# Recurrent heads of a hybrid block: PSUM sums in three sets of banks in turn instead of two

## The chip, the cores and the metric

The kernel runs on one core of one Trainium2 chip. Times are device microseconds (us) of the whole program, from one launch; lower is better. The core has TensorE (PE in the profile, with its weight loads as PEld), VectorE (DVE), ScalarE (ACT), GpSimd (POOL) and SyncE (SP, here a queue of DMA issues). TensorE writes its results into PSUM, 8 banks of 512 fp32 values per partition; ACT and DVE read them from there.

## The reference, cut to what matters

Two layers of a diffusion transformer over 1280 tokens (256 of context, 1024 latent), width 1024. The first layer has an S5 branch and a gated linear recurrence (RG-LRU) with 4 heads of 256 channels; the change is in the latter.

```python
# per head of 256 channels; h: [1280, 1024]
xr, gr = h @ w_xr, h @ w_gr                    # two projections
xc = centred_dwconv(xr, conv_w, conv_b)        # 4 taps over time
for d in (forward, backward):
    r  = sigmoid(xc @ wa[d] + ba[d])           # gates, 256x256 each
    ig = sigmoid(xc @ wx[d] + bx[d])
    a  = exp(-8 * r * softplus(-lam[d]))
    b  = sqrt(1 - a*a) * ig * xc
    h_t = a_t * h_(t-1) + b_t                  # a scan over the tokens
out = (forward + backward) * silu(gr)
```

## The kernel before

Each engine has a program written out by hand, with semaphores between them; nothing is reordered by a planner. The recurrent heads are one stage of the program, four heads one after another in a loop (`RH` = 4); they take about 442 us of the whole.

A head has twelve **sums** on PE. A sum is one tile of 128 channels by 1280 tokens, accumulated in PSUM in three pieces of 512, 512 and 256 tokens (`SEGS`), 2.5 banks in all. I number them j = 0 to 11 in the order of PE's program:

- sums 0 and 1: the projection `xr` for the two halves s of the head (8 steps of k for each piece, signal `rg_pmm`);
- sums 2 and 3: the projection `gr` (the same size);
- sums 4 to 11: for u = 0 to 3 (direction d, half s), the gate sums m = 0 (r) and m = 1 (ig), 2 steps of k for each piece, signal `rg_gmm`.

Even sums go to `ps3[0]` (banks 0, 1 and half of bank 2), odd sums to `ps3[1]` (banks 3, 4 and half of bank 5). Banks 6, 7 and the other halves of 2 and 5 are not used in this stage. PE may start sum j only when sum j-2 has been taken out of the same set: that is `pe.wait_ge` on `rg_ev0` or `rg_ev1` (lines 965 and 979). These two semaphores rise by 6 in each head: once by ACT's copy of sum 0 or 1, once by DVE's product of sum 2 or 3 with its own sigmoid, and four times by ACT's sigmoids of the gate sums.

What the other engines do for a head, in their program's order:

- ACT: waits for the end of the head before (`rg_bo`), because `xrp` and the gate `SG` lie in one place; copies sums 0 and 1 into `xrp` (L1554, L1555); waits for both halves of the convolution (`xc_ready`); takes the sigmoids of sums 2 and 3 (L1559); then for each u the two sigmoids of the gate sums (L1570), the square root for u-1 (L1562, in `root`), an exponential, a square and a tanh (L1574, L1578, L1579). Changes between these functions cost table loads.
- DVE: after the last product of the head before (L2297, signal `rg_bo`) 10 steps of the S5 scan (`scan_steps`, 4 small operations each, L2239 to L2244), the convolution of half 0 (L2260 to L2264), 8 steps, the convolution of half 1, 2 steps, the product of sum 2 with its sigmoid (L2269, `rg_ev0`), 1 step, the product of sum 3 (`rg_ev1`), 5 steps, and then for each u `gated(u)` (L2276, L2278) and `recurrence(u)` (L2287 and the token scans L2289 to L2297).
- POOL runs the other half of the S5 scan beside all that. SP loads weights.

PE waits for `xc_ready` and the gate weights before sum 4. After the last head PE goes on with `gate_rows` (banks 4 to 6, L1590 takes them) and `outputs`.

Of the kernel before, what the change touches and what calls it, by code (L numbers as in the profile page):

```python
# [17 lines left out]
ALU = mybir.AluOpType  # L18
ACT = mybir.ActivationFunctionType
AX = mybir.AxisListType  # L20

P = 128
BANK = 512
D = 1024
DT = D // P
CTX, LAT = 256, 1024
TOK = CTX + LAT
SEGS = [(0, 512), (512, 512), (1024, 256)]
# [10 lines left out]
NB = G // GB  # L39
# [8 lines left out]
RH, RD = 4, 256  # L48
# [9 lines left out]
LOFF = CTX + 3  # L58
# [45 lines left out]
def build(nc, A, out):  # L104
    with ExitStack() as ctx:
# [13 lines left out]
        def sem(name):  # L119
            name = lineage(name)[0]  # L120
            if name not in sems:
                sems[name] = ctx.enter_context(nc.semaphore(name))
            return sems[name]

        def past(name, n):

            return sem(name), n + lineage(name)[1]
# [7 lines left out]
        def mm(o, lhsT, rhs, k, n):  # L135
            return nc.tensor.matmul(o, lhsT, rhs, start=(k == 0), stop=(k == n - 1))  # L136
# [5 lines left out]

        psf = ps[:, :, :].rearrange("p b c -> p (b c)")
        ps3 = [psf[:, 3 * s * BANK:3 * s * BANK + TOK] for s in range(2)]

        def at(o, n):
            return AR[:, o:o + n]
# [5 lines left out]
        PV = sb("param_cols", 384)  # L153
# [13 lines left out]
        Wv = W[:, :].rearrange("p (s k n) -> p s k n", s=2, k=DT)  # L167
# [123 lines left out]
        xrp = rb(0, 2 * PAD).rearrange("p (s t) -> p s t", s=2)  # L291
        xcb = rb(2572, 2 * TOK).rearrange("p (s t) -> p s t", s=2)
# [5 lines left out]
        SG = rb(0, 2 * TOK).rearrange("p (s t) -> p s t", s=2)  # L298
# [25 lines left out]
        GWv = GW[:, :].rearrange("p (d m k n) -> p d m k n", d=2, m=2, k=2)  # L324
# [30 lines left out]
        HT = over("h_full", DT * TOK, AR0 + 4 * HTo, F32)[:, :].rearrange("p (k t) -> p k t", k=DT)  # L355
# [475 lines left out]
        def _(pe):  # L831
# [31 lines left out]
            for k in range(2, DT):  # L863
                c, h = 1 + (k - 2) // 2, 4 * (k % 2)
# [4 lines left out]
            for b in range(NBLK):  # L869
                last = mm(ps[:, 6, b:b + 1], sq_sum0[:, P * b:P * b + P], ones[:, 0:1], 0, 1)  # L870
            last.then_inc(sem("ss_mm0"), 1)
            pe.wait_ge(*past("mod_row", 5))
            for (c0, n), row in zip(MODC, mod_rows):
                for b in range(0, n, P):
                    g = 2 * ((c0 + b) // P)
                    last = nc.tensor.transpose(ps[:, 4, g:g + 2], row[:, b:b + P], ident[0:2, 0:2])
            last.then_inc(sem("mod_cols"), 1)
            pe.wait_ge(*past("diag0", 1))
            for b, (o, n) in ((0, (ps[:, 5, 0:CTX], 2)), (2, (ps[:, 6], 4)), (6, (ps[:, 7], 4))):
                last = mm(o, ones[:, :], diag0[:, b:b + n].rearrange("p b c -> p (b c)"), 0, 1)  # L880
# [18 lines left out]
            for k in range(DT):  # L899
                pe.wait_ge(*past("h_low", k + 1))  # L900
                for m in range(2):
                    last = u_product(m, k)
                    if k == DT - 1:
                        last.then_inc(sem(f"u_mm{m}"), 1)
            for m in range(2, DT):
                i, s = m // 2, m % 2
                pe.wait_ge(*past("u_wl", m - 1))
                pe.wait_ge(*past(f"u_ev{s}", i))
                for k in range(DT):
                    last = u_product(m, k)  # L910
# [16 lines left out]
            with pe.Fori(0, NB // 2) as i:  # L927
                for s in range(2):
# [3 lines left out]
                    for r in range(2):  # L932
                        for g in range(GB):
# [6 lines left out]
                            last = mm(ps[:, r, P * g:P * g + P], Xw[s][r][:, P * g:P * g + P], (nident, ident)[r][:, :], 1, 2)  # L940
                    last.then_inc(sem(f"x_t{s}"), 1)
                    for g in range(GB):
                        for d in range(2):
                            rw = slice(64 * d, 64 * d + 64)
                            for r in range(2):
                                last = mm(ps[0:HC, 6 + d, P * g:P * g + P], BBv[rw, s, r, :, g],
                                          Gv[s][rw, g, r, d:d + T, :], r, 2)
# [5 lines left out]
                    for r in range(2):  # L953
                        for g in range(GB):
                            last = mm(ps[:, 2 + 2 * r + g // 2, NJ * (g % 2):NJ * (g % 2) + NJ], Eg[:, r, g], Ub[s][:, g], 0, 1)
# [3 lines left out]
            pe.wait_ge(*past("h_back2", 3))  # L959

            def branch_head(i):
                for kind in range(2):
                    for s in range(2):
                        pe.wait_ge(*past(f"rg_w{s}", 32 * i + 16 * kind + 16))
                        pe.wait_ge(*past(f"rg_ev{s}", 6 * i + kind))
                        for t0, n in SEGS:
                            if isinstance(i, int) and kind == 0 and s == 0 and t0 == 1024:
                                pe.wait_ge(*past("wz_a", NB))
                                pe.wait_ge(*past("wz_v", NB))
                                pe.wait_ge(*past("v_ev", NB))  # L970
                            for k in range(DT):
                                last = mm(ps3[s][:, t0:t0 + n], Wv[:, s, k], HT[:, k, t0:t0 + n], k, DT)
                        last.then_inc(sem(f"rg_pmm{s}"), 1)
                pe.wait_ge(*past("rg_gw", 64 * i + 64))
                pe.wait_ge(*past("xc_ready", 2 * i + 2))
                for u in range(4):
                    d, s = u // 2, u % 2
                    for m in range(2):
                        pe.wait_ge(*past(f"rg_ev{m}", 6 * i + (2 + u)))
                        for t0, n in SEGS:  # L980
                            for k in range(2):
                                last = mm(ps3[m][:, t0:t0 + n], GWv[:, d, m, k, P * s:P * s + P], xcb[:, k, t0:t0 + n], k, 2)
                        last.then_inc(sem(f"rg_gmm{m}"), 1)

            branch_head(0)
            with pe.Fori(1, RH) as i:
# [2 lines left out]
            def gate_rows(i, z, js):  # L989
                for j in js:  # L990
                    t0, n = SEGS[j]
                    pe.wait_ge(*past(f"gs_w{z}", 16 * i + 16))
                    pe.wait_ge(*past(f"gs_ev{j}", 2 * i + z))
                    for k in range(DT):
                        last = mm(ps[:, 4 + j, 0:n], Wv[:, z, k], HT[:, k, t0:t0 + n], k, DT)
                    last.then_inc(sem(f"gs_mm{z}"), 1)
# [30 lines left out]
            def modulation_columns():  # L1027
# [6 lines left out]
                        last = mm(o, mod1_rows[z][:, x + P * t:x + P * t + P], quads[:, 0:n], 0, 1)  # L1034
                last.then_inc(sem("mod1_cols"), 1)

            gate_rows(0, 0, (2,))
            pe.wait_ge(*past("rg_ev0", 6 * RH))
            pe.wait_ge(*past("rg_ev1", 6 * RH))
# [25 lines left out]
            with pe.Fori(0, DT // 2) as i:  # L1065
                for s in range(2):
                    pe.wait_ge(*past("glu_wl", 2 * i + (s + 1)))
                    pe.wait_ge(*past(f"glu_sz{s}", i))
                    for k in range(DT):
                        pe.wait_ge(*past("y_low", k + 1))  # L1070
                        last = three_parts(ps3[s], WPs[s], YTs, k, DT)
# [72 lines left out]
            for k in range(DT):  # L1144
                pe.wait_ge(*past("ht1_low", k + 1))
                for s in range(2):
                    for q, (a, b) in enumerate(PARTS):
                        for j, (t0, n) in enumerate(XSEGS[s]):
                            last = mm(psP[s][j], WXs[s][:, a, k], HTs[b][:, k, t0:t0 + n], 3 * k + q, 3 * DT)
# [9 lines left out]
            for g in range(GQ):  # L1159
                last = nc.tensor.matmul(quarter(g), WFs[:, 0, 0], X2[:, 0, GN * g:GN * g + GN], start=True, stop=False, skip_group_check=True)  # L1160
# [244 lines left out]
        def _(act):  # L1405
# [144 lines left out]
            with act.Fori(0, RH) as i:  # L1550
                act.wait_ge(*past("rg_bo", 2 * i))
                for s in range(2):
                    act.wait_ge(*past(f"rg_pmm{s}", 2 * i + 1))
                    nc.scalar.activation(xrp[:, s, 1:1 + CTX], ps3[s][:, 0:CTX], ACT.Copy)  # L1554
                    nc.scalar.activation(xrp[:, s, LOFF + 1:LOFF + 1 + LAT], ps3[s][:, CTX:TOK], ACT.Copy).then_inc(sem(f"rg_ev{s}"), 1)  # L1555
                act.wait_ge(*past("xc_ready", 2 * i + 2))
                for s in range(2):
                    act.wait_ge(*past(f"rg_pmm{s}", 2 * i + 2))
                    nc.scalar.activation(SG[:, s], ps3[s], ACT.Sigmoid).then_inc(sem("rg_sg"), 1)  # L1559
                def root(u):  # L1560
                    act.wait_ge(*past("rg_om", 4 * i + (u + 1)))
                    nc.scalar.activation(RT[:, u % 2], RT[:, u % 2], ACT.Sqrt).then_inc(sem("rg_sq"), 1)  # L1562

                for u in range(4):
                    d, s = u // 2, u % 2
                    if u >= 2:
                        act.wait_ge(*past("rg_dir", 4 * i + (u - 1)))
                    for m, (dst, c0) in enumerate(((RT, C_BA), (IT, C_BX))):
                        act.wait_ge(*past(f"rg_gmm{m}", 4 * i + (u + 1)))
                        nc.scalar.activation(dst[:, s], ps3[m], ACT.Sigmoid, bias=PV[:, bass.ds(2 * i + (c0 + 8 * d + s), 1)]).then_inc(sem(f"rg_ev{m}"), 1)  # L1570
                    if u:
                        root(u - 1)
                    act.wait_ge(*past("rg_ev0", 6 * i + (3 + u)))
                    nc.scalar.activation(AT[:, s], RT[:, s], ACT.Exp, scale=lamc[:, bass.ds(2 * i + (8 * d + s), 1)]).then_inc(sem("rg_at"), 1)  # L1574
                    act.wait_ge(*past("rg_at", 12 * i + (3 * u + 1)))
                    if u:
                        act.wait_ge(*past("rg_om", 4 * i + u))
                    nc.scalar.activation(TT[:, 0:TOK], AT[:, s], ACT.Square).then_inc(sem("rg_at"), 1)  # L1578
                    nc.scalar.activation(RT[:, s], RT[:, s], ACT.Tanh, scale=lamc[:, bass.ds(2 * i + (16 + 8 * d + s), 1)]).then_inc(sem("rg_at"), 1)  # L1579
                root(3)  # L1580
# [237 lines left out]
            for m in range(MT):  # L1818
# [5 lines left out]
                if m == 0:  # L1824
# [6 lines left out]
                    for n, r in enumerate((rLI, rLF)):  # L1831
                        nc.scalar.activation(r[0:32], psG[64 * n:64 * n + 32], ACT.Identity, bias=BI[64 * n:64 * n + 32, :])
                        for o, x in zip(natural(r, slice(32, 64)), (psG[64 * n + 32:64 * n + 64, 0:CTX], psG[64 * n + 32:64 * n + 64, CTX:TOK])):
                            last = nc.scalar.activation(o, x, ACT.Identity, bias=BI[64 * n + 32:64 * n + 64, :])
# [130 lines left out]
        def _(dve):  # L1965
            V = nc.vector
# [20 lines left out]
            for q in range(24):  # L1987
                t0, n = SEGS[q % 3]
# [135 lines left out]
            f, bk = slice(0, 64), slice(64, 128)  # L2124
# [100 lines left out]
            with dve.Fori(0, RH) as i:  # L2225
                k, step = [0], [0]
# [39 lines left out]
                for s in range(2):  # L2266
                    scan_steps(1)
                    dve.wait_ge(*past("rg_sg", 2 * i + s + 1))
                    V.tensor_tensor(SG[:, s], ps3[s], SG[:, s], ALU.mult).then_inc(sem(f"rg_ev{s}"), 1)  # L2269
                scan_steps(5)  # L2270

                def gated(u):
# [149 lines left out]
            with dve.Fori(0, MT // 2) as i:  # L2422
                k = [0]
# [583 lines left out]
```

## Time and profile before

| | us |
|---|---|
| time, median of 3 runs (lowest to highest) | 2696.11 (2691.78 to 2697.48) |
| the profiled execution: its time | 2691.36 |
| its span, first to last instruction | 2689.7 |
| mean granted clock of TensorE | 0.983 of 2.4 GHz |
| PE busy | 2550.7 (95% of the span) |
| DVE / ACT / POOL busy | 1530.1 / 827.5 / 988.3 |

The profiled execution lies at the fast end of the runs; 1.7 us of its time lie outside its span. A share of busy time is a mean over stages with different limits, so the stage of the heads is read by itself. An fp32 matmul shows as two records. The line of most matmuls is L136, a helper, so they are told apart by their operands: `h_full,weights` are the projections, `arena,weights` 128x128 are the gate sums.

### The profile page before, as it was taken

To read this page: it belongs to the slowest core of one execution; us is meant where nothing else is said; L and a number is where in the kernel's file an instruction comes from. 1 tells how busy PE (TensorE), PEld (TensorE's weight loads), DVE (VectorE), ACT (ScalarE), POOL (GpSimd) and SP (SyncE) were. 2 spreads that over 40 slices of the span, in tenths; PEclk is the share of its full clock that TensorE was granted. 3 is DMA by queue.
4 is the path that set the end of the run, shared out by engine and by line. 5 is a ranking of instruction groups with operands and counts; after the bars stand their busy time and mean duration, and the time that the engine had idled before them with its cause. 6 is when DMAs were issued, how large, how long until landed. Compare 5 with 4: busy or idle time off the path is not lost.

```text
span 2689.7 us, 37273 instructions
## 1 busy us (share of the span) xinstructions
PE 2550.7 (95%) x13319; PEld 1979.7 (74%) x13319; DVE 1530.1 (57%) x2359; ACT 827.5 (31%) x994; POOL 988.3 (37%) x1162
## 2 busy tenths in 40 slices
PE   7898899999999998999999999998999999999998
PEld 3787854545455667888877887777989889898787
DVE  3677765887875225524246664966465555646510
ACT  2425635263552113312122112123233241422210
POOL 0139967887800100211224433445334333331000
PEclk9999999999999999999989999999999999999999
DMA  7413320111106785351132333564131321215421
GB/s 295 121 57 92 97 76 27 48 32 43 51 16 215 252 266 157 100 183 36 36 98 95 124 117 125 177 230 153 44 116 54 106 88 63 100 35 173 133 94 47
DMA packets 272083, 293.95 MB, mean 109 GB/s; under 512 B 35232, under 2 KB 234184, under 8 KB 271568
## 3 DMA queue, kind: packets, MB, share of 16 engines
q1 hardware_dynamic: 202672, 209.75, 24.3%
q10 hardware_dynamic: 64672, 65.70, 7.4%
q0 software_dynamic: 4608, 16.78, 1.9%
q8 instruction: 79, 1.29, 0.2%
q14 instruction: 52, 0.43, 0.1%
HBM read 200.99 MB, written 91.20 MB: 109 GB/s over the span
## 4 chain that ended last, share of the span: by engine, by line
PE 69%; DVE 9%; issue 3%; ACT 3%; DMA 2%; POOL 1%; ACTq 0%; SPq 0%; DVEq 0%; POOLq 0%
PE ps L136 61%; PE ps L1372 6%; DVE xc_part L2536 1%; PE ps L1023 1%; ACT arena L1570 1%; DVE arena L2464 1%; ACT L1570 1%; DMA ml_z<-arena 0%; PE ps L1377 0%; DVE arena L528 0%; PE ps L1305 0%; DMA qk_map_full<-ml_qk_maps 0%; DVE arena L2453 0%; PE ps L1203 0%; DVE arena L2465 0%
## 5 line engine op out<-in xcount | busy, mean ns | idle before, releaser
L136 PE MATMUL ps<-h_full,weights 128*128 128x512 f32 (+1 forms) x1152 | 417.8, 523 | 8.7 <-ACT arena L1570 4.0
L136 PE MATMUL ps<-h_part,in_weight_parts 128*128 128x512 f32 (+1 forms) x1920 | 412.8, 376 | 13.7 <-POOL in_weight_parts L2879 6.5
L136 PEld LDWEIGHTS ps<-h_part,in_weight_parts 128*128 128x128 f32 x1920 | 337.0, 190 | 84.6 <-issue 8.1
L136 PEld LDWEIGHTS ps<-h_full,weights 128*128 128x128 f32 x1152 | 218.3, 190 | 201.5 <-issue 187.0
L136 PE MATMUL ps<-v_part,p_part 128*128 128x512 f32 x1248 | 296.7, 396 | 0.1
L136 PEld LDWEIGHTS ps<-v_part,p_part 128*128 128x128 f32 x1248 | 235.4, 191 | 49.6 <-issue 0.8
L136 PE MATMUL ps<-q_part,xc_part 128*128 128x256 f32 x1920 | 244.4, 286 | 3.9 <-DVE q_part L2569 3.9
L136 PEld LDWEIGHTS ps<-q_part,xc_part 128*128 128x128 f32 x1920 | 234.1, 192 | 4.9 <-DVE q_part L2569 4.5
L136 PE MATMUL ps<-arena,weights 64*16 64x128 f32 (+2 forms) x896 | 177.3, 388 | 16.0 <-ACT arena L1570 14.4
L1372 PE MATMUL ps<-wo_part,mx_part 128*128 128x512 f32 x768 | 183.9, 400 | 5.2 <-DVE mx_part L2536 4.8
L2873 POOL TENSOR_TENSOR in_weight_parts<-weights,ones 128x1024 fp32r<-128x1024 f32 x32 | 81.3, 2541 | 258.3 <-PE ps L136 188.0
L1372 PEld LDWEIGHTS ps<-wo_part,mx_part 128*128 128x128 f32 x768 | 145.4, 191 | 39.8 <-issue 5.0
L2959 POOL TENSOR_TENSOR decays<-decays,p_full 128x256 f32<-128x256 f32 (+1 forms) x128 | 150.6, 1177 | 60.4 <-DVE p_full L2647 34.8
L136 PEld LDWEIGHTS ps<-arena,weights 64*16 64x16 f32 (+1 forms) x896 | 101.1, 144 | 89.4 <-issue 64.3
L2375 DVE SCALAR_TENSOR_TENSOR arena<-ps,modulation,arena 128x256 f32 (+3 forms) x32 | 32.6, 1061 | 164.5 <-PE ps L136 160.6
L136 PE MATMUL ps<-y_part,out_weight_parts 128*128 128x512 f32 (+1 forms) x576 | 113.0, 358 | 3.5 <-DVE y_part L2321 2.3
L136 PE MATMUL ps<-bo_part,out_weight_parts 128*128 128x512 f32 (+1 forms) x576 | 114.6, 359 | 0.0
L136 PE MATMUL ps<-ao_part,out_weight_parts 128*128 128x512 f32 (+1 forms) x576 | 114.4, 358 | 0.0
L136 PEld LDWEIGHTS ps<-y_part,out_weight_parts 128*128 128x128 f32 x576 | 95.0, 188 | 21.4 <-DVE y_part L2321 2.7
L136 PEld LDWEIGHTS ps<-ao_part,out_weight_parts 128*128 128x128 f32 x576 | 95.3, 188 | 16.9
L136 PEld LDWEIGHTS ps<-bo_part,out_weight_parts 128*128 128x128 f32 x576 | 95.3, 188 | 16.9
L136 PE MATMUL ps<-arena 128*128 128x160 f32 (+4 forms) x620 | 98.2, 297 | 6.4 <-DMA arena<-s_lags 6.0
(396 smaller groups left out, 4119.1 us busy)
## 6 DMA issues: line engine op xcount, KB each, us to landing
weights<-in_e_w_in SPq DMA_DIRECT2D x32, 512.0 KB, 5.1
weights<-in_o_w_in SPq DMA_DIRECT2D x32, 512.0 KB, 4.5
arena<-in_mod_w POOLq DMA_DIRECT2D x24, 512.0 KB, 5.6
ml_xcv<-arena ACTq DMA_DIRECT2D x16, 640.0 KB, 2.9
xc_full<-ml_xcv SPq DMA_DIRECT2D x4, 2560.0 KB, 10.5
xm_tiles<-ml_xm SPq DMA_DIRECT2D x15, 640.0 KB, 3.8
arena<-in_mod_w SPq DMA_DIRECT2D x4, 2048.0 KB, 21.3
s_out_maps<-arena ACTq DMA_DIRECT2D x32, 256.0 KB, 3.3
```

The source lines that it names most:

```text
L136: return nc.tensor.matmul(o, lhsT, rhs, start=(k == 0), stop=(k == n - 1))
L1023: last = nc.tensor.matmul(ps[32 * g:32 * g + 32, 7, o:o + MN], csw[:, k], modw1[n % 3][:, x:x + MN], start=(n % MU1 == 0), stop=(k == DT - ...
L1372: nc.tensor.matmul(ps[:, 2 * (b % 4) + h], Mbs[x][b % 2][:, k], Wos[w][k][:, BANK * h:BANK * h + BANK], start=(k == 0 and n == 0), stop=Fa ...
L1570: nc.scalar.activation(dst[:, s], ps3[m], ACT.Sigmoid, bias=PV[:, bass.ds(2 * i + (c0 + 8 * d + s), 1)]).then_inc(sem(f"rg_ev{m}"), 1)
L2375: V.scalar_tensor_tensor(out=o, in0=a, scalar=MOD[:, bass.ds(4 * i + (2 * (16 + s) + w), 1)], in1=x, op0=ALU.mult, op1=ALU.add).then_inc(s ...
L2464: V.scalar_tensor_tensor(out=bst2[:, s], in0=xcz[:, s], scalar=PV[:, C_SK + m:C_SK + m + 1], in1=zo[:, s], op0=ALU.mult, op1=ALU.mult)
L2536: V.tensor_tensor(o, x, h.bitcast(F32), ALU.subtract).then_inc(sem(name), 1)
L2873: GP.tensor_tensor(WXs[s][:, 0], Wv[:, s], ones[:, :].unsqueeze(1).to_broadcast([P, DT, P]), ALU.mult).then_inc(sem("w_high"), 1)
L2959: GP.tensor_tensor(Sp[:, z, s0:s1], Sp[:, z, s0:s1], PR[:, z, o:o + s1 - s0], ALU.add).then_inc(sem("sums"), 1)
```

## The change

The sums of a head take three sets of banks in turn. Set A (j mod 3 = 0) begins in the second half of bank 5 and covers banks 6 and 7; set B (j mod 3 = 1) is banks 0, 1 and half of 2, set C (j mod 3 = 2) banks 3, 4 and the first half of 5. So sets A and C share bank 5, each with a piece of 256 tokens; in set A the order of pieces is 256-767, 768-1279, 0-255, so that in both the piece in the shared bank comes third. Sum j starts when sum j-3 has been taken. Before its third piece a sum in set A also waits until sum j-1 (set C) has been taken, and a sum in set C until sum j-2 (set A) has been. ACT gets two waits for the first gate sums (u = 0), and the rows after the last head one more. ACT and DVE read the sums from their new places; no operation is added, removed or put elsewhere in their order.

```diff
+        RG_AT = (5 * BANK + 256, 0, 3 * BANK)
+        rg_ps = [psf[:, RG_AT[j % 3]:RG_AT[j % 3] + TOK] for j in range(12)]
+        RG_SEGS = [((256, 512), (768, 512), (0, 256)), SEGS, SEGS]
...
             def branch_head(i):
+                def sums_taken(j):
+                    c = (j % 12 if j < 0 else j) // 2 + (1 if j >= 0 else -5)
+                    if not (isinstance(i, int) and 6 * i + c <= 0):
+                        pe.wait_ge(*past(f"rg_ev{j % 2}", 6 * i + c))
+
+                def rg_sums(j, product, steps):
+                    sums_taken(j - 3)
+                    for x, (t0, n) in enumerate(RG_SEGS[j % 3]):
+                        if x == 0 and isinstance(i, int) and i == 0 and j == 0:
+                            pe.wait_ge(*past("v_ev", NB))
+                        if x == 2 and isinstance(i, int) and i == 0 and j == 0:
+                            pe.wait_ge(*past("wz_a", NB))
+                            pe.wait_ge(*past("wz_v", NB))
+                        if x == 2 and j % 3 == 0:
+                            sums_taken(j - 1)
+                        if x == 2 and j % 3 == 2:
+                            sums_taken(j - 2)
+                        for k in range(steps):
+                            w, v = product(k, t0, n)
+                            last = mm(rg_ps[j][:, t0:t0 + n], w, v, k, steps)
+                    return last
...
-                        pe.wait_ge(*past(f"rg_ev{s}", 6 * i + kind))
...
+                        rg_sums(2 * kind + s, lambda k, t0, n: (Wv[:, s, k], HT[:, k, t0:t0 + n]), DT).then_inc(sem(f"rg_pmm{s}"), 1)
...
-                        pe.wait_ge(*past(f"rg_ev{m}", 6 * i + (2 + u)))
...
+                        rg_sums(4 + 2 * u + m, lambda k, t0, n: (GWv[:, d, m, k, P * s:P * s + P], xcb[:, k, t0:t0 + n]), 2).then_inc(sem(f"rg_gmm{m}"), 1)
...
+            pe.wait_ge(*past("rg_ev1", 6 * RH - 1))
             gate_rows(0, 0, (2,))
...
-                    nc.scalar.activation(SG[:, s], ps3[s], ACT.Sigmoid).then_inc(sem("rg_sg"), 1)
+                    nc.scalar.activation(SG[:, s], rg_ps[2 + s], ACT.Sigmoid).then_inc(sem("rg_sg"), 1)
...
+                        if u == 0:
+                            act.wait_ge(*past(f"rg_ev{m}", 6 * i + 2))
-                        nc.scalar.activation(dst[:, s], ps3[m], ACT.Sigmoid, bias=...
+                        nc.scalar.activation(dst[:, s], rg_ps[4 + 2 * u + m], ACT.Sigmoid, bias=...
...
-                    V.tensor_tensor(SG[:, s], ps3[s], SG[:, s], ALU.mult).then_inc(sem(f"rg_ev{s}"), 1)
+                    V.tensor_tensor(SG[:, s], rg_ps[2 + s], SG[:, s], ALU.mult).then_inc(sem(f"rg_ev{s}"), 1)
```

## Rows read from the trace of the kernel before

**Rows 1.** Busy time by engine, stretches of one head; the second head and the sum of four.

```profile
core 0: us, PE busy (x) PEld busy (x) DVE busy (x) ACT busy (x) POOL busy (x), PEclk, DMA share, GB/s
469.50:581.50 112.00, 108.39 (x288) 56.12 (x288) 92.86 (x201) 52.59 (x43) 90.33 (x180) 0.95 0.11 36
...
sum 442.00, PE 421.83 PEld 220.32 DVE 336.01 ACT 198.91 POOL 306.17; mean PE 105.46 PEld 55.08 DVE 84.00 ACT 49.73 POOL 76.54
```

**Rows 2.** Waits in the stage (359 to 806 us): total, times, longest.

```profile
PE ps L136 <- ACT arena L1570: 18.5, 10, 2.8
...
PE ps L136 <- DVE arena L2269: 1.5, 1, 1.5
```

**Rows 3.** PE in order of time: start, duration, line, operands, records, idle before.

```profile
359.16 68.98 PE L136 MATMUL ps<-h_full,weights 128*128 128x512 f32 x192 [2.65 <-DMA weights<-in_e_w_in]
427.98 17.35 PE L136 MATMUL ps<-arena,weights 128*128 128x512 f32 x48
446.13 8.86 PE L136 MATMUL ps<-arena,weights 128*128 128x512 f32 x24 [0.80 <-ACT arena L1570]
457.80 8.86 PE L136 MATMUL ps<-arena,weights 128*128 128x512 f32 x24 [2.81 <-ACT arena L1570]
...
540.02 17.35 PE L136 MATMUL ps<-arena,weights 128*128 128x512 f32 x48
...
652.06 17.45 PE L136 MATMUL ps<-arena,weights 128*128 128x512 f32 x48 [1.54 <-DVE arena L2269]
...
762.50 17.35 PE L136 MATMUL ps<-arena,weights 128*128 128x512 f32 x48
...
801.01 3.62 PE L136 MATMUL ps<-h_full,weights 128*128 128x256 f32 x16
...
820.64 17.42 PE L136 MATMUL ps<-h_full,weights 128*128 128x512 f32 x48 [1.42 <-ACT weights L1590]
```

**Rows 4.** ACT in order of time, gate sums of the first head.

```profile
444.75 2.54 ACT L1570 ACTIVATE arena<-ps,param_cols 128x1280 f32<-128x1280 f32 x2
...
456.42 2.55 ACT L1570 ACTIVATE arena<-ps,param_cols 128x1280 f32<-128x1280 f32 x2
...
460.28 1.27 ACT L1562 ACTIVATE arena<-arena 128x1280 f32<-128x1280 f32 x1
```

**Rows 5.** DVE in order of time, ends of heads and products of sums 2.

```profile
413.60 1.49 DVE L2269 TENSOR_TENSOR arena<-ps,arena 128x1280 f32<-128x1280 f32 x1 [9.21 <-ACT arena L1559]
...
461.58 1.49 DVE L2287 TENSOR_TENSOR arena<-arena 128x1280 f32<-128x1280 f32 x1 [0.44 <-ACT arena L1562]
...
496.40 1.49 DVE L2297 TENSOR_TENSOR arena<-arena 128x1280 f32<-128x1280 f32 x1
...
538.27 1.48 DVE L2269 TENSOR_TENSOR arena<-ps,arena 128x1280 f32<-128x1280 f32 x1
...
573.62 1.49 DVE L2287 TENSOR_TENSOR arena<-arena 128x1280 f32<-128x1280 f32 x1
...
608.68 1.49 DVE L2297 TENSOR_TENSOR arena<-arena 128x1280 f32<-128x1280 f32 x1
...
650.53 1.48 DVE L2269 TENSOR_TENSOR arena<-ps,arena 128x1280 f32<-128x1280 f32 x1
...
720.83 1.49 DVE L2297 TENSOR_TENSOR arena<-arena 128x1280 f32<-128x1280 f32 x1
...
760.66 1.48 DVE L2269 TENSOR_TENSOR arena<-ps,arena 128x1280 f32<-128x1280 f32 x1
```

**Rows 6.** POOL's half of the S5 scan, last operation of a step.

```profile
L2810 POOL TENSOR_TENSOR arena<-arena,s_scan_tmp x160: 316/318/2590, 363.3 to 745.4; 128x64 f32 x160
```

**Rows 7.** Stretches behind an idle PE: length, PE busy (records), granted clock.

```profile
469.47:476.00 6.53, 6.53 (x12) 0.74 0.27 84
...
569.84:577.00 7.16, 7.16 (x11) 0.57 0.00 0
...
681.98:686.00 4.02, 4.02 (x6) 0.60 0.00 0
```

**Rows 8.** PE in order of time, behind its longest idle time after the stage.

```profile
1016.21 5.21 PE L136 MATMUL ps<-arena 128*128 128x160 f32 x24 [5.99 <-DMA arena<-s_lags]
```

More of the change, by code:

```diff
@@ L964, in branch_head @@
                         pe.wait_ge(*past(f"rg_w{s}", 32 * i + 16 * kind + 16))
-                        pe.wait_ge(*past(f"rg_ev{s}", 6 * i + kind))
[L966 to L973, printed above, removed]
+                        rg_sums(2 * kind + s, lambda k, t0, n: (Wv[:, s, k], HT[:, k, t0:t0 + n]), DT).then_inc(sem(f"rg_pmm{s}"), 1)
                 pe.wait_ge(*past("rg_gw", 64 * i + 64))
@@ L978, in branch_head @@
                     for m in range(2):
-                        pe.wait_ge(*past(f"rg_ev{m}", 6 * i + (2 + u)))
[L980 to L983, printed above, removed]
+                        rg_sums(4 + 2 * u + m, lambda k, t0, n: (GWv[:, d, m, k, P * s:P * s + P], xcb[:, k, t0:t0 + n]), 2).then_inc(sem(f"rg_gmm{m}"), 1)
             branch_head(0)
@@ L1553, in _ @@
                     act.wait_ge(*past(f"rg_pmm{s}", 2 * i + 1))
-                    nc.scalar.activation(xrp[:, s, 1:1 + CTX], ps3[s][:, 0:CTX], ACT.Copy)
-                    nc.scalar.activation(xrp[:, s, LOFF + 1:LOFF + 1 + LAT], ps3[s][:, CTX:TOK], ACT.Copy).then_inc(sem(f"rg_ev{s}"), 1)
+                    nc.scalar.activation(xrp[:, s, 1:1 + CTX], rg_ps[s][:, 0:CTX], ACT.Copy)
+                    nc.scalar.activation(xrp[:, s, LOFF + 1:LOFF + 1 + LAT], rg_ps[s][:, CTX:TOK], ACT.Copy).then_inc(sem(f"rg_ev{s}"), 1)
                 act.wait_ge(*past("xc_ready", 2 * i + 2))
@@ L1569, in _ @@
                         act.wait_ge(*past(f"rg_gmm{m}", 4 * i + (u + 1)))
-                        nc.scalar.activation(dst[:, s], ps3[m], ACT.Sigmoid, bias=PV[:, bass.ds(2 * i + (c0 + 8 * d + s), 1)]).then_inc(sem(f"rg_ev{m}"), 1)
+                        if u == 0:
+                            act.wait_ge(*past(f"rg_ev{m}", 6 * i + 2))
+                        nc.scalar.activation(dst[:, s], rg_ps[4 + 2 * u + m], ACT.Sigmoid, bias=PV[:, bass.ds(2 * i + (c0 + 8 * d + s), 1)]).then_inc(sem(f"rg_ev{m}"), 1)
                     if u:
```

## The prediction

> **What bounds the kernel now.** The page first: PE is busy 95% of the span, so I look for where PE is late. The stretches of the heads come next [rows 1]: over the four heads (442 us) PE is busy 421.8 us, so about 20 us are idle, and that is all that a change of buffers can win here. The view of waits says what ends this idle time [rows 2]: ten times ACT's sigmoid of a gate sum, 18.5 us together, and once DVE's product L2269, 1.5 us. The time lines then show the order. In the first head PE's projections run from 359.16 to 427.98 without a gap, 17.2 us a sum; sums 4 to 7 follow, 17.35 us for four, so 4.3 us each; then PE waits 0.80 us before sum 8, 2.81 us before sum 10, and 2.8 us again before the next head's first sum [rows 3]. Behind these waits is ACT: its pairs of sigmoids start at 444.75 and 456.42, one u in 11.67 us, where PE needs 8.6 us for a pair [rows 3, 4].
>
> PE alone is not the whole bound. I call G the start of sum 4. G is at 427.98, 540.02, 652.06 and 762.50 in the four heads [rows 3]: 112.0, 112.0 and 110.4 us apart. A second loop, through DVE, is as long. From G to the end of the head (L2297) it takes 608.68 + 1.49 - 540.02 = 70.15 us, from there to the end of DVE's product of sum 2 (538.27 + 1.48, or 650.53 + 1.48) 41.85 us, together 112.0 us [rows 3, 5]. In the third head this loop is the one that closes: PE starts sum 4 at 652.06, 0.05 us after DVE's product ended, having waited 1.54 us for it [rows 3, 5]. In the other two the product was done only 0.3 us before G (539.75 against 540.02; 762.14 against 762.50). So DVE's product of sum 2 is always just in time now. Only in the first head is it early (415.1).
>
> **The change part by part.** I go through the sums and ask of each wait whether it is over in time.
>
> *Sums 8 and 10, and the next sum 0.* Sum 8 now needs sum 5 taken (before 444.75) at its start, and sum 6 taken (444.75 + 1.28 = 446.03) for its third piece. It starts at 445.3, its third piece is due 3.4 us later: the 0.80 us go. Sum 10 needs sum 7, taken at 447.3, and the next head's sum 0 needs sum 9. Their own waits of 2.8 us go as well.
>
> *Sum 9, the third piece.* It lies in bank 5 beside sum 8 and waits until ACT has taken sum 8. PE gets there at 427.98 + 5 x 4.3 + 3.4 = 452.9; ACT has sum 8 out at 456.42 + 1.28 = 457.7 [rows 4]. So PE stands 4.9 us here, in place of twice 2.8. The piece (a fifth of 4.3 us, 0.86) then ends at 458.65, and ACT, which took sum 9 right behind sum 8, at 457.75, can start it 0.3 us after that, at about 458.95: ACT is 1.2 us late from here. Queued behind it on ACT are the square root of u = 1 and all that follows. DVE's L2287 waits for that root in the first head (0.44 us), and in the second it starts at 573.62 with no slack to speak of [rows 4, 5]. So the end of the head comes 1.2 us later, counted from G. If the clock is low when PE restarts, the piece takes 0.86 us more: 2.05 us.
>
> *Sum 3, the third piece.* Sum 3 is in set A, and its third piece waits until sum 2, in set C, has been taken. What takes sum 2 is not ACT, it is DVE's product L2269, which stands in DVE's program behind both convolutions. Before the change PE needed that product at G, when all of sum 3 was done. Now it needs it one piece earlier. The piece is 16 of 48 records; a fifth of 17.2 us is 3.43, and a piece of that size elsewhere took 3.62 [rows 3]. Since the product is just in time now, G comes 0.05 + 3.43 us after it. The first head is spared: there the product is done 9 us before the piece is due. This wait adds 3.5 us to the loop through DVE in heads 2, 3 and 4, and nothing hides it, since PE has no other work in its order.
>
> *The clock.* Where PE stood for 2.8 us it came back at the low level (1.2 GHz) three times of eight or nine: 12, 11 and 6 records at a granted clock of 0.74, 0.57 and 0.60, which lost 6.53 x 0.26 = 1.7, 7.16 x 0.43 = 3.1 and 1.6 us [rows 7]. Behind the 5.99 us of idle time 24 records took 5.21 us, which the same 24 do in 3.5 with a full clock: 1.7 us lost [rows 8]. In sum 3 PE will now stand longer than that: PE alone gets from G to the next third piece in about 106 us and must wait for 114. I take 1.7 us for each such stop; bounds are 0 and 3.1. For sum 9 I take the low clock too (2.05 us). The Trainium skill (TensorE: Matmul & The Clock Gate, The HAM clock gate) says that the clock has two levels and falls to half of the full rate when TensorE has been idle, which rows 7 and 8 agree with.
>
> *The rest.* The new waits of ACT for the products of sums 2 and 3 are over when the gate sums arrive (the product of sum 3 ends 3.0 us after G, sum 5 ends 8.6 after it): 0. The third piece of sum 5 (needs sum 3 taken) is due 7.7 us after G: 0. Sums 0, 2, 6, 8 and 11 have slack of at least a microsecond. `v_ev` one piece earlier in the first head: PE stands for weights there until 359.16 anyhow. Loads on SP wait for the same signals and have 17 us of a projection to land. The wait before `gate_rows` is for sum 9, long taken. Reading a sum from another offset costs the same: every 128x1280 read is in one piece.
>
> **The sum**, from the profiled execution.
> Head 2: end of head 1 at 497.89, + 2.05 = 499.94; + 41.86 for DVE to its product = 541.80; + 0.05 + 3.43 + 1.7 gives G = 546.98, against 540.02: +7.0.
> Head 3: 546.98 + 70.15 + 2.05 + 41.84 + 5.18 = 666.2, against 652.06: +14.1.
> Head 4: DVE's way to the product is 39.8 us there, 2.0 less, since POOL's half of the scan ends at 745.4 and DVE's steps are quicker without it [rows 5, 6]. The head now begins later, so more steps run free: I take 2 us more (bounds 0 and 3). 666.2 + 70.26 + 2.05 + 37.8 + 5.18 = 781.5, against 762.50: +19.0.
> Behind the heads: + 2.05 for sum 9 once more, +21.1. PE's next piece of work at 820.64 waits for ACT's L1590, which waits for DVE [rows 3]: it moves with DVE's chain, and from there PE is without a gap.
> With no loss by the clock: 4.4, 9.0, 11.3, and +12.5 at the end. With 3.1 us per stop and no relief by POOL: about +27.
> On the profiled 2691.4 us that is 2712; on the median of the runs, 4.7 us higher, 2717. I give **2716 us**.
>
> **The rivals.**
> *The gates decide (no change, or faster).* The product of sum 2 would have to be out before the third piece of sum 3 is due, that is 3.5 us or more earlier after G than in rows 3 and 5. Then PE has its 103 us of matmuls, 4.9 us at sum 9 and the clock: 107.9 to 109.6 against 112.0, but DVE's loop of 112.0 + 1.2 stays above that. So even then it is no gain beyond the clock; if DVE's loop were 4 us shorter than I read it, 2 to 5 us in all: 2691 to 2694. For it: PE's 18.5 us of waits are real. Against: the rows of L2269. Chance 0.08. In the Trainium skill (Perfetto Trace Analysis, Matmuls) independent groups should rotate through different banks so that taking one out overlaps the next; by that rule alone the change gains. Here two groups still meet in bank 5, and its page PSUM — Partial Sum Buffer (bank collisions) wants guards by bank, which is what the two extra waits do.
> *The stall comes, but small.* DVE's steps run faster once PE and ACT stand, or POOL ends much earlier: 1 to 3 us less per head, +3 to +11, 2700 to 2707. Chance 0.09.
> *The clock stays low.* Each stop costs over 3.1 us, or sum 9's stop delays ACT further: +27 to +35, 2724 to 2731. Chance 0.05.
> My forecast has the rest, 0.78.
>
> **How the numbers follow.** A difference of 0.2%, 5.4 us, is about what a measurement of this kernel can tell from none. Faster: a quarter of the first rival, 0.02. Same: the rest of it and a little of the second, 0.08. Slower: 0.90. Low end: +12.5 on the fastest run is 2704, and the second rival reaches below, so 2702. High end: +27 on the median is 2723, so 2725.
>
> **What the profile of after would show.** G in the four heads at about 428, 547, 666 and 781. PE idle inside the group of the 192 projection records of heads 2 to 4, 3 to 8 us, released by DVE L2269, with 16 records behind it up to G and a clock below 1. Idle of some 5 us inside the gate sums, released by ACT L1570 with about 2 gate matmuls (4 records) left in the sum; none of 0.8 us before sum 8. ACT's two sigmoids of u = 2 apart by 1.2 to 2 us instead of back to back. The prediction is wrong if L2269 in heads 2 to 4 ends more than 3.4 us before G, or if G's distances are under 112.

## The result and the profile after

| | before | after |
|---|---|---|
| median of 5 runs, us | 2696.11 (2691.78 to 2699.29) | 2714.68 (2713.58 to 2721.31) |
| profiled span, us | 2689.7 | 2713.0 |
| mean granted clock | 0.983 | 0.976 |

The ratio is 1.008, with a 95% interval of 1.0063 to 1.0097: 17 to 26 us slower. The forecast was 2716 us, between 2702 and 2725, and "slower" at 0.9.

PE in order of time, of the kernel after (start, duration, line, operands, records, idle before), answers to [rows 3]:

```profile
360.68 68.98 PE L136 MATMUL ps<-h_full,weights 128*128 128x512 f32 x192 [2.50 <-DMA weights<-in_e_w_in]
429.50 25.08 PE L136 MATMUL ps<-arena,weights 128*128 128x512 f32 x68
459.32 12.57 PE L136 MATMUL ps<-arena,weights 128*128 128x256 f32 x28 [4.74 <-ACT arena L1587]
...
543.19 5.59 PE L136 MATMUL ps<-h_full,weights 128*128 128x256 f32 x16 [6.01 <-DVE arena L2286]
548.62 25.08 PE L136 MATMUL ps<-arena,weights 128*128 128x512 f32 x68
...
662.37 5.73 PE L136 MATMUL ps<-h_full,weights 128*128 128x256 f32 x16 [5.90 <-DVE arena L2286]
667.94 25.08 PE L136 MATMUL ps<-arena,weights 128*128 128x512 f32 x68
...
777.53 3.72 PE L136 MATMUL ps<-h_full,weights 128*128 128x256 f32 x16 [3.37 <-DVE arena L2286]
781.09 25.08 PE L136 MATMUL ps<-arena,weights 128*128 128x512 f32 x68
...
841.62 17.42 PE L136 MATMUL ps<-h_full,weights 128*128 128x512 f32 x48 [0.96 <-ACT weights L1607]
```

The waits of 0.80 and 2.81 us are gone; what stands in their place is larger. Sixty-eight records run from G without a stop: sums 4 to 8 and two pieces of sum 9. Then PE stands 4.74 us before the last four records of sum 9. And in heads 2 to 4 it stands 6.01, 5.90 and 3.37 us before the last 16 records of sum 3, until DVE's product (L2286 here, L2269 before). G is at 429.50, 548.62, 667.94 and 781.09: 119.1, 119.3 and 113.2 us apart, where it was 112.0, 112.0 and 110.4 [rows 3].

The waits of PE in the stage (359 to 830 us; total, times, longest), where [rows 2] had 18.5 us in ten waits for ACT and 1.5 for DVE:

```profile
PE ps L136 <- ACT arena L1587: 19.0, 4, 4.7
PE ps L136 <- DVE arena L2286: 15.3, 3, 6.0
```

The wait for ACT is as long in all as it was, in four stops instead of ten, and the one for DVE is new.

ACT at sums 8 and 9 of the first head, to be held against [rows 4], where both sigmoids stood in one row back to back:

```profile
457.94 1.33 ACT L1587 ACTIVATE arena<-ps,param_cols 128x1280 f32<-128x1280 f32 x1
461.54 1.33 ACT L1587 ACTIVATE arena<-ps,param_cols 128x1280 f32<-128x1280 f32 x1 [2.27 <-PE ps L136]
```

ACT stands 2.27 us for sum 9. DVE's second L2304 (L2287 before) had waited 0.44 us for ACT's root in the first head. Now it waits 2.37 us. Its row stands first here, then DVE's ends of heads and its products of sum 2, which answer to [rows 5]:

```profile
465.48 1.54 DVE L2304 TENSOR_TENSOR arena<-arena 128x1280 f32<-128x1280 f32 x1 [2.37 <-ACT arena L1577]
...
499.82 1.49 DVE L2314 TENSOR_TENSOR arena<-arena 128x1280 f32<-128x1280 f32 x1
...
541.66 1.48 DVE L2286 TENSOR_TENSOR arena<-ps,arena 128x1280 f32<-128x1280 f32 x1
...
738.25 1.49 DVE L2314 TENSOR_TENSOR arena<-arena 128x1280 f32<-128x1280 f32 x1
...
776.00 1.48 DVE L2286 TENSOR_TENSOR arena<-ps,arena 128x1280 f32<-128x1280 f32 x1
```

From the first G to the end of the head it takes 501.31 - 429.50 = 71.81 us (497.89 - 427.98 = 69.91 before), from there to the end of the product 41.83 (41.86 before), and PE starts 0.05 us later: the loop is the one the prediction drew, with two things put into it.

### The profile page after: what moved, and what is told of

Read it like the earlier page. It is cut to its first block, busy times and chain, and to the rows that moved or that the text cites. A ratio compares the mean times of both kernels' runs of the same rounds, so it can differ in the third digit from the quotient of the medians.

```text
span 2713.0 us, 37285 instructions
## 1 busy us (share of the span) xinstructions
PE 2560.1 (94%) x13319; PEld 1987.9 (73%) x13319; DVE 1530.2 (56%) x2359; ACT 827.4 (30%) x994; POOL 988.7 (36%) x1162
## 4 chain that ended last, share of the span: by engine, by line
PE 63%; DVE 13%; issue 5%; ACT 4%; DMA 2%; POOL 1%; DVEq 0%; ACTq 0%; SPq 0%; POOLq 0%
PE ps L136 55%; PE ps L1387 6%; DVE s_scan_tmp L2259 1%; DVE arena L2261 1%; DVE s_scan_tmp L2257 1%; DMA ml_z<-arena 1%; DVE arena L2279 1%; DVE xc_part L2553 1%; DVE arena L2311 1%; PE ps L1037 1%; DVE arena L2304 1%; PE ps L1392 0%; PE ps L1320 0%; DVE arena L531 0%; ACT arena L1591 0%
```

## Experiments

The theory: two waits for the shared bank carry the loss, that of sum 3 for DVE and that of sum 9 for ACT. The rivals are that the third set costs by itself (half banks, piece order, ACT's two waits), or the clock does it.

**One wait at a time, with the two old sets.** In the kernel before, a wait in front of one piece:

```diff
                         for t0, n in SEGS:
...
+                            if kind == 1 and s == 1 and t0 == 1024:          # e1_wait3
+                                pe.wait_ge(*past("rg_ev0", 6 * i + 2))
...
+                            if u == 2 and m == 1 and t0 == 1024:             # e2_wait9
+                                pe.wait_ge(*past("rg_ev0", 6 * i + 5))
```

> The kernel before with one wait more: the third piece of sum 3 waits for DVE's product of sum 2. Two sets as before, no shared bank. Theory: this wait by itself carries most of the loss. G (start of sum 4) 5 us later in head 2, 10 in head 3, 14 in head 4, and 10 to 17 us in all; PE idle behind DVE L2269 in the middle of the last projection of heads 2 to 4. Rival (the third set itself costs, by the shared bank or the two new waits of ACT): no change, within 3 us of before.

> The kernel before with one wait more: the third piece of sum 9 waits until ACT has taken sum 8. Theory: ACT gets sum 9 some 2 us late in each head, DVE has no slack there, and G moves by 2, 4 and 6 us, 5 to 9 us in all, so that with the wait of sum 3 the two make up what the change lost. Rival (PE merely stands here instead of before sum 10, and ACT and DVE have slack): within 2 us of before.

> The kernel before, two sets, with both waits added (sum 3 for DVE's product, sum 9 for ACT's sigmoid of sum 8). Theory: the two make up the whole loss of the changed kernel: 15 to 24 us above before, G 117 to 120 us apart. Rival (they overlap, or a third cause is in the new banks): under 13 us.

The last column is the length of the stage in the profiled execution, from the first G to the start of the piece that [rows 3] show at 820.64. What differs ahead of the stage is left out of it. Each ratio is to runs of the kernel before that were taken beside it.

| | median us | ratio to before (95%) | G apart, us | stage, us (more than before) |
|---|---|---|---|---|
| before | 2696.11 | | 112.0, 112.0, 110.4 | 392.7 |
| wait of sum 3 | 2706.53 | 1.0038 (1.0024 to 1.0052) | 117.0, 115.9, 112.0 | 403.1 (10.4) |
| wait of sum 9 | 2705.14 | 1.0041 (1.0025 to 1.0056) | 113.7, 113.7, 114.3 | 402.2 (9.6) |
| both | 2717.43 | 1.0075 (1.0059 to 1.0090) | 118.9, 118.9, 114.1 | 412.5 (19.8) |
| after | 2714.68 | 1.0080 (1.0063 to 1.0097) | 119.1, 119.3, 113.2 | 412.1 (19.5) |

PE in order of time, of the kernel with the wait of sum 3 alone, in head 2:

```profile
544.06 5.09 PE L136 MATMUL ps<-h_full,weights 128*128 128x256 f32 x16 [5.03 <-DVE arena L2271]
548.99 17.35 PE L136 MATMUL ps<-arena,weights 128*128 128x512 f32 x48
```

and of the one with the wait of sum 9 alone, heads 2 and 3:

```profile
542.09 17.45 PE L136 MATMUL ps<-arena,weights 128*128 128x512 f32 x48 [0.85 <-DVE arena L2271]
...
572.01 11.42 PE L136 MATMUL ps<-arena,weights 128*128 128x256 f32 x28 [3.67 <-ACT arena L1572]
...
655.77 17.45 PE L136 MATMUL ps<-arena,weights 128*128 128x512 f32 x48 [1.64 <-DVE arena L2271]
```

The same 16 records of sum 3 stand behind DVE, in heads 2 and 3. With sum 9's wait PE has its stop of 3.67 us there, and in heads 2 and 3 it then waits for DVE's product before sum 4: DVE has fallen behind PE. Each wait costs about 0.4%, both 0.75%, and the changed kernel 0.8%; in the stage it is 10.4 and 9.6 us, and 19.8 together. No third set is in these kernels, so the two waits are enough for the whole loss; the rival that they overlap, or that the new banks cost, falls.

Two things had been expected otherwise. The wait of sum 3 was to carry most of the loss (G 5, 10 and 14 us later); it carries half (5.0, 8.8 and 10.4 us). And in head 4 of all three kernels PE does not wait for DVE at all: it comes to G without a stop, still late from its stops in head 3's gate sums and before the next sum 0. So with two sets the last head loses by another way than in the changed kernel, where PE stands 3.37 us for the product.

**The reader made early.** In the changed kernel, the sigmoid and the product of sum 2 go between the two convolutions:

```diff
-                act.wait_ge(*past("xc_ready", 2 * i + 2))
                 for s in range(2):
+                    act.wait_ge(*past("xc_ready", 2 * i + s + 1))
                     act.wait_ge(*past(f"rg_pmm{s}", 2 * i + 2))
...
                     dve.wait_ge(*past("xc_ready", 2 * i + s))
+                    if s == 1:
+                        dve.wait_ge(*past("rg_sg", 2 * i + 1))
+                        V.tensor_tensor(SG[:, 0], rg_ps[2], SG[:, 0], ALU.mult).then_inc(sem("rg_ev0"), 1)
```

> The changed kernel with DVE's product of sum 2 put ahead of the convolution of half 1, and ACT's sigmoid of sum 2 after the convolution of half 0. Theory: the third piece of sum 3 finds sum 2 taken, its stall goes in all heads, the stall of sum 9 stays; G 110 to 112 us apart, 16 to 20 us less than the changed kernel, within 4 us of before. Rival (clock or shared bank, not this wait): it stays 10 us or more above before.

Measured: 2701.26 us, ratio 1.0014 (1.0000 to 1.0029); G 112.3, 112.0 and 110.1 us apart, as before the change. PE in order of time, at G of head 2 and at sum 9:

```profile
544.42 25.18 PE L136 MATMUL ps<-arena,weights 128*128 128x512 f32 x68 [1.20 <-DVE arena L2284]
574.35 12.63 PE L136 MATMUL ps<-arena,weights 128*128 128x256 f32 x28 [4.74 <-ACT arena L1587]
```

The stop in sum 3 is gone with the three sets and the shared bank in place, that of sum 9 is there still. 13.4 us came back by the medians, where I had expected 16 to 20, and the result is 5 us above before, a little over what I had given; its ten runs spread from 2689 to 2707 us, wider than those of the others. The stage in the profiled execution is 395.0 us, 17.1 less than in the changed kernel and 2.3 more than before. The 2.3 us come behind the last G, where sum 9 still stands.

**The sets given out in another order.** Same banks, same shared bank, same guards; what changes is which sum takes which set, and with it the order of a sum's pieces and the wait before `gate_rows`:

```diff
-        rg_ps = [psf[:, RG_AT[j % 3]:RG_AT[j % 3] + TOK] for j in range(12)]
+        RG_AT = {"A": 5 * BANK + 256, "B": 0, "C": 3 * BANK}
+        RG_SET = "ABABCABCABCB"
+        rg_ps = [psf[:, RG_AT[x]:RG_AT[x] + TOK] for x in RG_SET]
...
+        def rg_last(j, x):
+            return max(q for q in range(j - 12, j) if RG_SET[q % 12] == x)
...
-                    sums_taken(j - 3)
+                    sums_taken(rg_last(j, RG_SET[j]))
...
+                        if x == 2 and RG_SET[j] != "B":
+                            sums_taken(rg_last(j, {"A": "C", "C": "A"}[RG_SET[j]]))
```

> Three sets as in the changed kernel, in the same banks with the same shared bank and pieces, but given out as A B A B C A B C A B C B instead of A B C four times, so that no third piece waits for a late reader: sum 3 is in B, sum 9 in B. Theory: both stalls go, sum 4 no longer needs DVE's product, the loop through DVE is 108.3 us; G 108 to 110 us apart and 5 to 10 us less than before, 2686 to 2691. Rival (three sets can't gain, the shared bank or ACT's waits cost by themselves): above 2696.

The 108.3 us are the way from G to the end of the head (70.15) and from there to the end of the second convolution, which PE waits for before sum 4. In the kernel before that is at 534.62 + 1.34 = 535.96, 38.1 us after the end of head 1:

```profile
534.62 1.34 DVE L2264 SCALAR_TENSOR_TENSOR arena<-arena,param_cols 128x1024 f32<-128x1024 f32 x1
```

Measured: 2691.33 us, ratio 0.9981 (0.9972 to 0.9990). G was 110.6, 110.4 and 111.1 us apart, not 108 to 110. It is faster than before, so neither the shared bank nor ACT's two waits are what cost 19 us. It won less than the loop allowed. Its profiled execution is the slowest of its eleven (2699.63 us), so its rows may show more loss than the median has. DVE in order of time shows where up to 2 us a head went:

```profile
508.66 0.22 DVE L2258 TENSOR_TENSOR s_scan_tmp<-arena,s_decay 128x64 f32<-128x64 f32 x1
510.76 0.39 DVE L2259 TENSOR_TENSOR s_scan_tmp<-arena,s_decay 128x64 f32<-128x64 f32 x1 [1.88 <-issue]
```

DVE stands 1.88 us (2.05 and 1.75 in the next two heads) between two small operations that need nothing of each other, waiting for nothing that the profile shows. On the queue of SP in the same kernel:

```profile
502.66 0.37 SPq L577 DMA_DIRECT2D rg_out<-arena  x1
503.07 0.47 SPq L593 DMA_DIRECT2D weights<-in_e_w_in  x1
```

The store of the head's output (1280 KB) and a weight load (512 KB) are issued 0.4 us apart. Before, they were 7.9 us apart, as PE came to the end of sum 1 later. So I moved the store behind sum 2:

```diff
-                    if i and s == 0:
-                        branch_out(i - 1)
+                if i:
+                    sp.wait_ge(*past("rg_pmm0", 2 * i + 2))
+                    branch_out(i - 1)
```

> The sets given out as A B A B C A B C A B C B, and besides the store of the head before moved behind sum 2 on the queue of SP. In the run with these sets DVE stood 1.9 to 2.1 us at the fourth step of its scan in heads 2 to 4, waiting for nothing in the profile, while the store (1280 KB) and a weight load (512 KB) filled the DMA engines. Theory: the fetch of DVE's instructions waits behind them; with the store later the gap goes, G 108.5 to 109 us apart in place of 110.4, 3 to 6 us less: 2683 to 2688. Rival (the gap belongs to the code, not to the DMAs): it stays, 2690 to 2692.

Measured: 2688.57 us, ratio 0.9969 (0.9957 to 0.9982); G 109.4, 109.3 and 109.3 us apart, both a little above what I had given. The gap is gone from the profile: DVE's waits for nothing fell from 5.7 us at L2259 and 4.9 at the head's first memset to the 4.9 alone. The two medians are only 2.8 us apart and their intervals overlap, so the gain in time is less certain than the gap. That it was the fetch of DVE's instructions that stood behind the data is a reading and not shown. The queue of SP in this kernel also narrows it:

```profile
524.52 0.37 SPq L577 DMA_DIRECT2D rg_out<-arena  x1
524.93 0.47 SPq L583 DMA_DIRECT2D weights<-in_e_w_in  x1
```

The store is again issued 0.4 us before a weight load of 512 KB, 22 us later in the head, and the DMA engines move up to 374 GB/s behind it; DVE works on through that (0.77 to 0.93 busy in each microsecond from 524 to 532). So two transfers together do not stop DVE by themselves. DVE stood for 2 us only where they met the fourth step of its scan; what is special there is open.

What is left between 108.3 and 109.3 us is a stop of PE of 3.1 to 3.2 us before sum 2, which follows sum 0 in set A and so needs ACT's copy of sum 0. That copy waits for the end of the head before, and from there PE runs to G without a stop.

**Two more orders, and the clock.**

> As the run with the late store, with the sets in the order A B C B A C A B C B C B: sum 2 no longer follows sum 0 in its set, so PE doesn't stand 2 to 3 us before sum 2, but all its slack falls before sum 4 (5 to 6 us). Theory: the loop through DVE sets the time, G the same distance apart; if the clock is low behind the longer stop, sums 4 and 5 run slow and ACT gets them up to 1.7 to 3 us late, so 0 to 6 us more than the run with the late store. Rival (PE sets the time): 2 to 6 us less.

> Late store, and the sets in the order A B C B A C B C A B C B: no sum follows its own set at a distance at which the reader is late, neither sum 2 (3 us) nor sum 10 (3.9 us). Theory: PE then needs about 104 us a head, DVE's loop of 108.3 us sets the time, and the clock stays high in the gate sums: G 108.3 to 108.7 apart, 2 to 4 us less than the two runs with the late store: 2683 to 2688. Rival (what is left of PE's slack falls before sum 4, with the clock low behind it): G 109 to 110.5 apart and the same time as they.

| with the late store | median us | ratio to before (95%) | G apart, us |
|---|---|---|---|
| A B A B C A B C A B C B | 2688.57 | 0.9969 (0.9957 to 0.9982) | 109.4, 109.3, 109.3 |
| A B C B A C A B C B C B | 2690.98 | 0.9980 (0.9970 to 0.9989) | 110.1, 108.6, 110.2 |
| A B C B A C B C A B C B | 2687.54 | 0.9970 (0.9958 to 0.9982) | 108.1, 110.3, 109.9 |

In the second order PE did not stand 5 to 6 us before sum 4, as I had expected, but 1.14 us in one head and not at all in the others. It stood 3.9 us before sum 10 in each head. In heads 1 and 3 it came back at the low level (24 records in 11.70 and 11.37 us, granted clock 0.75 and 0.78 over them), and PE then set the time, G 110.1 and 110.2 us apart. In head 2 it came back at the high level from the same stop, and G followed after 108.6 us:

```profile
567.86 8.86 PE L136 MATMUL ps<-arena,weights 128*128 128x512 f32 x24 [3.88 <-ACT arena L1590]
```

The time was within the 0 to 6 us that I had given, but not for the reason given. PE in order of time, of the last of the three orders, heads 2 to 4, shows what limits that one:

```profile
536.13 31.14 PE L136 MATMUL ps<-arena,weights 128*128 128x512 f32 x80 [3.69 <-DVE arena L2284]
...
646.46 32.28 PE L136 MATMUL ps<-arena,weights 128*128 128x512 f32 x80 [4.22 <-DVE arena L2284]
...
756.35 29.48 PE L136 MATMUL ps<-arena,weights 128*128 128x512 f32 x80 [2.63 <-DVE arena L2284]
```

Eighty records take 29.5 us at the high clock. Behind stops of 3.69 and 4.22 us they took 1.7 and 2.8 us more, and this is at the head of the gate sums, where ACT waits for each. From G to the end of the head it took 69.9 us in head 1, where PE had not stopped, and 72.2 and 72.8 us in heads 2 and 3. So the first distance is 108.1 us, as the loop says, and the next two are 110.3 and 109.9. Both the theory (108.3) and its rival (109 to 110.5) are seen, in different heads of one run. The three orders differ by less than I can tell.

Twice I tried to hold the clock up with throwaway matmuls:

```diff
+                        if x == 2 and j == 3 and not isinstance(i, int):      # e5_fill, in the changed kernel
+                            sums_taken(1)
+                            for r in range(5):
+                                mm(rg_ps[1][:, 0:512], Wv[:, 1, r], HT[:, r, 0:512], 0, 1)
...
+                if not isinstance(i, int):                                    # e8_hold, in e7_order
+                    sums_taken(rg_last(4, RG_SET[4]))
+                    for r in range(4):
+                        mm(rg_ps[4][:, 256:768], GWv[:, r % 2, 0, 0, 0:P], HT[:, r, 0:512], 0, 1)
```

> The changed kernel with five throwaway matmuls of 512 columns in heads 2 to 4, between the second and third piece of sum 3, into the free set B: PE works for 4.3 us of the 3 to 6 us that it would stand. The waits stay as they are. Theory of the clock term: the third piece of sum 3 then takes 3.4 us instead of 5.3 in heads 2 and 3, G comes 1.9 and 3.8 us earlier there, while head 4, which stood only 3.4 us, loses about 1: 2 to 4 us less than the changed kernel. Rival (the clock isn't on the path): the same or 1 us slower.

> As the run before, with four throwaway matmuls of 512 columns (3.4 us) before sum 4 in heads 2 to 4, into the set that sum 4 will take. Theory: PE's slack is filled, the clock stays at its high level for the gate sums, G unchanged but the heads 1 to 3 us shorter behind it: 3 to 6 us less than without, 2680 to 2686. Rival (low clock costs nothing here): no change, or 1 to 3 us slower where there was no slack.

The first: 2717.18 us, ratio 1.0087 (1.0062 to 1.0111), no gain. PE in order of time, of that kernel:

```profile
542.07 5.41 PE L136 MATMUL ps<-h_full,weights 128*128 128x256 f32 x16 [3.03 <-DVE arena L2290]
...
662.08 5.41 PE L136 MATMUL ps<-h_full,weights 128*128 128x256 f32 x16 [3.95 <-DVE arena L2290]
```

PE still stood 3.0 and 4.0 us, more than the 1.7 that I had left over, as the heads' earlier stops had cost less here, and the clock was low again; in head 4 it did not stand, and G came 114.2 us after the last, 1.0 more than in the changed kernel, as expected. So this run does not measure the clock term. The second: 2700.86 us, ratio 1.0021 (1.0011 to 1.0031), G 113.5, 112.4 and 113.2 us apart. It added 3.0 to 3.8 us a head: in that order PE had next to no slack to fill, as sum 10 stood 3.9 us and the clock behind it took the rest. The expectation was wrong there; PE, not DVE, set the time of that kernel.

## Why the prediction was right

- *The product of sum 2 in the loop.* Right: +3.5 us a head for the piece. The kernels with this wait alone and with the reader made early show that the wait is the cause, and the rows of the kernel after show the size, 3.56 us from the piece to G in head 4, at the high clock. PE starts the piece 0.05 us after the product in all three heads.
- *Sum 9.* Foreseen 4.9 us of PE and 2.05 of ACT; measured 4.74 and 2.27. (The two sigmoids were to stand 1.2 to 2 us apart.) From G to the end of the head it took 71.8 us in each of the three heads, 1.9, 1.7 and 1.5 us more than before, where 2.05 was added each time. So DVE made good 0.2 to 0.5 us that the forecast had put at nothing.
- *The clock.* Sized 1.7 us for each stop in sum 3. The count behind it was wrong: [rows 2] and the rows of PE have five stops of 2.8 us in the stage, so three low returns were three of five, not of eight or nine. In heads 2 and 3 the 16 records took 5.59 and 5.73 us against 3.72 in head 4: 1.9 and 2.0 us. In head 4, behind 3.37 us, the clock stayed up and the term is 0: that is 1.6 of the 2.1 us by which G came earlier than forecast (113.2 us and not 115.3), and the end of the head is the rest. The sign that was to be seen, a clock below 1 in heads 2 to 4, held in two of three. The windows of the kernel after say the same (length, PE busy with records, granted clock):

```profile
541.00:549.00 8.00, 5.81 (x17) 0.62 0.00 0
660.00:668.00 8.00, 5.63 (x17) 0.60 0.00 0
776.00:781.10 5.10, 3.56 (x17) 1.00 0.00 0
```

  The Trainium skill (TensorE: Matmul & The Clock Gate, The HAM clock gate) says that the clock falls to half of the full rate when TensorE has been idle. The trace agrees in heads 2 and 3 (0.62 and 0.60); in head 4 the clock stayed at 1.00 behind 3.37 us of idle time.
- *POOL's relief* of 2 us in head 4: end of head 739.74 to end of product 777.48 is 37.7 us; 37.8 forecast.
- *The sum.* The piece at 820.64 [rows 3] is at 841.62, +21.0, where +21.1 was forecast; but 1.5 us of that lie ahead of the stage (it began at 360.68, not at 359.16), so the stage gave 19.5. The medians give 18.6. The excess of the forecast is head 4's clock; the other terms were off by up to 0.5 us each, some up and some down, and cancel. That 21.0 stands beside 21.1 is luck. Behind that piece the profiled execution lost another 2.3 us against the one before (23.3 in all), which the forecast had at nothing and no row here explains.
- *The gain at the gates* was worth nothing, as forecast: PE's own waits went, and DVE's loop stood above them. In the first rival I had written that DVE's loop would have to be shorter; the other order of sets made it so, since sum 4 no longer waits for the product, and there the gain appears.

## What to carry to other kernels

Before adding a buffer, ask of each new wait which engine takes the data out and where that stands in its program. A half bank shared between neighbours in the rotation brings a wait for the neighbour's reader one piece earlier than the old wait; it hurts where that reader sits late in a busy engine's order (the product of sum 2 on DVE), and where the reader is the engine that PE runs ahead of (ACT at sum 8). The set that each tile takes is a free choice: given out by when each reader is done, the same banks won 0.2%, and 0.3% with the store moved as well, where the plain rotation lost 0.8%.

## What had not been expected

Moving PE earlier brought a store and a weight load together, and DVE stood 1.8 to 2.1 us in each of three heads, waiting for nothing in the profile; with the store 22 us later this was gone. Short stops of PE can cost more than their length when they lie ahead of work on the path: 3.7 and 4.2 us of idle time were followed by 1.7 and 2.8 us of loss. Their length alone does not say which will: stops of 2.6, 3.4 and 3.9 us were followed by none, and three of five stops of 2.8 us in the kernel before by some [rows 7].
